# Half of a unit's gate-weighted one-hots are multiplied by their gates on ACT instead of DVE

## What is computed

```
idx = take(i1, ia) * 128 + take(i2, ib)            # (i, j) of each slot
gates = softmax(vals)
h = einsum('tkd,td->tk', expert_u[idx], x)
a = gelu(h) * gates
out = einsum('tk,tkd->td', a, expert_v[idx])
```

## Time and profile before

| | us |
|---|---|
| median of 3 runs (2219.46 to 2220.31) | 2220.23 |
| the profiled execution, its own time | 2217.2 |
| its span | 2215.4 |

### The profile page before, as it was taken

One profiled execution on the slowest core, in us unless ns is written; L12 is line 12 of the kernel. 1 busy time (PEld: TensorE's weight loads), 2 busy tenths in 40 slices (PEclk: granted clock), 3 DMA queues, 4 the chain that ended last, 5 costly groups with the idle time before them and its releaser, 6 DMA issues.

```text
span 2215.4 us, 35977 instructions
## 1 busy us (share of the span) xinstructions
PE 2127.0 (96%) x12658; PEld 1842.3 (83%) x12658; DVE 1250.9 (56%) x2110; ACT 977.1 (44%) x1406; POOL 126.1 (6%) x65
## 2 busy tenths in 40 slices
PE   7999996899999999999999999999999999999998
PEld 6998995656888888888888888787888888899997
DVE  4457799788666666666675333322645433355553
ACT  5644553223555555555564222212434334346652
POOL 0000676000000000000000000000000000000000
PEclk9999998999999999999999999999999999999999
DMA  6344453588555555556553333232233245254552
GB/s 220 125 133 162 135 169 114 201 292 275 191 191 188 189 186 186 188 203 194 188 173 116 98 100 99 95 100 90 78 112 112 85 143 174 100 186 138 185 188 96
DMA packets 95559, 343.24 MB, mean 155 GB/s; under 512 B 10915, under 2 KB 12451, under 8 KB 95109
## 3 DMA queue, kind: packets, MB, share of 16 engines
q1 hardware_dynamic: 94388, 337.28, 45.6%
q0 software_dynamic: 1104, 5.05, 0.6%
HBM read 341.24 MB, written 1.05 MB: 155 GB/s over the span
## 4 chain that ended last, share of the span: by engine, by line
PE 85%; DVE 10%; issue 2%; DMA 1%; ACT 1%; DVEq 0%; ACTq 0%; SPq 0%
PE ps L1418 14%; PE ps L1419 14%; PE ps L1420 14%; PE ps L1647 8%; PE ps L1661 5%; PE ps L1663 5%; PE ps L1662 5%; PE ps L1649 4%; PE ps L1449 2%; PE ps L1451 2%; PE ps L1450 2%; PE ps L1622 2%; PE ps L1598 1%; PE ps L1801 1%; DMA RAW<-in_wstream 1%
## 5 line engine op out<-in xcount | busy, mean ns | idle before, releaser
L832 DVE TENSOR_TENSOR WL<-RAW,WH 128x1024 fp32r<-128x1024 f32 x519 | 627.0, 1223 | 504.4 <-ACT WH L420 500.9
L420 ACT ACTIVATE WH<-RAW 128x1024 fp32r<-128x1024 f32 x565 | 585.0, 1053 | 285.8 <-PE ps L1420 159.7
L1418 PE MATMUL ps<-XH,WH 128*128 128x256 f32 (+1 forms) x1200 | 385.0, 321 | 7.0 <-DVE XL L849 5.3
L1419 PE MATMUL ps<-XL,WH 128*128 128x256 f32 (+1 forms) x1200 | 379.5, 316 | 0.0
L1420 PE MATMUL ps<-XH,WL 128*128 128x256 f32 (+1 forms) x1200 | 379.4, 316 | 0.0
L1647 PE MATMUL ps<-XHL,WH 128*128 128x512 f32 x752 | 268.5, 397 | 0.0
L1418 PEld LDWEIGHTS ps<-XH,WH 128*128 128x128 f32 x1200 | 229.3, 191 | 25.9 <-issue 5.4
L1419 PEld LDWEIGHTS ps<-XL,WH 128*128 128x128 f32 x1200 | 229.7, 191 | 15.5 <-issue 1.0
L1420 PEld LDWEIGHTS ps<-XH,WL 128*128 128x128 f32 x1200 | 229.6, 191 | 14.3
L1418 PE MATMUL ps<-XHL,WH 128*128 128x256 f32 x696 | 207.1, 298 | 24.9 <-POOL WL L391 11.4
L1649 PE MATMUL ps<-XHL,WL 128*128 128x256 f32 x752 | 210.9, 280 | 0.0
(11 more groups left out here) (276 smaller groups left out, 3153.1 us busy)
## 6 DMA issues: line engine op xcount, KB each, us to landing
RAW<-in_wstream SPq DMA_DIRECT2D x637, 512.0 KB, 3.4
H<-in_xT SPq DMA_DIRECT2D x1, 1024.0 KB, 4.8
CTX<-in_ctxT POOLq DMA_DIRECT2D x1, 1024.0 KB, 6.8
HX<-in_ctxT POOLq DMA_DIRECT2D x1, 1024.0 KB, 6.0
DIST<-in_dist POOLq DMA_DIRECT2D x1, 1024.0 KB, 5.1
out<-HX SPq DMA_DIRECT2D x2, 512.0 KB, 3.1
MASK<-in_mask POOLq DMA_DIRECT2D x1, 512.0 KB, 3.9
DFTL<-in_dftl POOLq DMA_DIRECT2D x1, 512.0 KB, 3.7
```

The source lines that it names most:

```text
L420: act.activation(WH[:, slot, :], RAW[:, slot, :], ACT.Copy).then_inc(hi_ready, 1)
L832: dve.tensor_tensor(WL[:, slot, :], RAW[:, slot, :], WH[:, slot, :].bitcast(F32), ALU.subtract).then_inc(lo_ready, 1)
L1418: pe.matmul(dst, wh, xh, start=start, stop=False, skip_group_check=not check)
L1419: pe.matmul(dst, wh, xl, start=False, stop=False, skip_group_check=not check)
```

## The change

A constant `FUSED = 4` splits a unit's 8 tokens. DVE still compares for `OJ`. For tokens 4 to 7 it then writes plain one-hots, 0 or 1, into `OI` with one compare of 512 elements and signals `hot_ready`; for tokens 0 to 3 it compares and multiplies as before and signals `onehot_ready`. ACT multiplies the four plain one-hots in place, each by its slot gates: four instructions (Copy with a scale per partition out of `SLT`), then `weighed`. This is `weigh(n)`. It stands on ACT ahead of the copy of the tables of the unit before: `weigh(0)`, `weigh(1)`, copy(0), `weigh(2)`, copy(1), and so on. PE waits for `weighed` of unit n as well.

```
+FUSED = 4
...
+            def weigh(n):
+
+                act.wait_ge(s["hot_ready"], n + 1)
+                for t in range(FUSED, 8):
+                    ins = act.activation(OI[n % 2][:, t, :], OI[n % 2][:, t, :], ACT.Copy,
+                                         scale=SLT[:, 2, 8 * n + t:8 * n + t + 1])
+                ins.then_inc(s["weighed"], 1)
+
             act.sem_inc(s["g_ready"], 2)
             done = 0
+            weigh(0)
             for n in range(UNITS):
+                if n + 1 < UNITS:
+                    weigh(n + 1)
                 act.wait_ge(s["onehot_used"], n + 3)
...
-                for t in range(8):
+                half = [P, 8 - FUSED, P]
+                dve.tensor_tensor(OI[q][:, FUSED:8, :], IOTA[:, :].unsqueeze(1).to_broadcast(half),
+                                  SLT[:, 0, 8 * n + FUSED:8 * n + 8].unsqueeze(2).to_broadcast(half),
+                                  ALU.is_equal).then_inc(s["hot_ready"], 1)
+                for t in range(FUSED):
...
                 pe.wait_ge(s["onehot_ready"], n + 1)
+                pe.wait_ge(s["weighed"], n + 1)
```

## The result

| | before | after |
|---|---|---|
| median, us (20 runs each) | 2219.85 (2214.83 to 2223.62) | 2223.04 (2220.39 to 2226.98) |
| the profiled execution, us | 2217.2 | 2222.95 |
| its span, us | 2215.4 | 2221.2 |
| the stage, from the last hidden copy to the first expert product, us | 405.79 to 539.82: 134.03 | 405.50 to 542.61: 137.11 |

The changed kernel takes 1.0017 of the time before, with a 95% interval of 1.001 to 1.0024: slower by a little, 0.17%, inside the 0.2% that were called "same" ahead. Forecast were 2224.2 us and 1.0018.

The account below looks back on a forecast made before the run. PE and its loads (4.10 us a unit) bound the stage; the change replaces them by an ACT and DVE loop of 4.20. +2.9 us, plus 1.1 for long loads, makes +4.0: 2224.2 us (1.0018), range 2220.6 to 2229.0.

Parts of the forecast that it names:

- What bounds the stage: Stage from 403 to 538 us: PE and its loads set 4.10 us a unit; DVE is busy but not waited for.
- DVE's own price: DVE before the change: eight L1111 in 2.13 us, own minimum 3.62 us a unit; the change saves 0.47 a unit.
- The price of a weighing: ACT's multiply of one one-hot by its gates: 0.29 us apart, four 1.16, or 1.26 with the last one's tail.
- the rival of 0.19 us: Cheap weighing on ACT: 0.19 us each, loop 3.80, below PE's 4.10; only the start stays, 2221 us; chance 0.16.
- The compare of four tokens: DVE's new compare of 512 elements: 0.68 us by itself, counted as 0.60 in a row of several.
- The loop: ACT and DVE wait for each other in the stage: 4.20 us a unit, 0.11 more with a row_sum.
- The rival of adding delays: In the stage, late loads for PE add to the ACT and DVE loop's delays: +8 us, 2228 us; chance 0.19.
- Start: Unit 0 on PE waits for the first weighings: starts at 407.4 us instead of 406.58, +0.8 us.
- End: Unit 31: OJ compare at 534.2 us, one-hots ready for PE at 537.4 against 534.50 before, +2.9 us.
- The term for long loads: Two long load legs in the stage stick out of the loop's slack by 1.2 and 0.4 us; +1.1 us taken.
- The absolute time: Whole kernel: profiled execution 2217.2 + 4.0 = 2221.2 us, median 3.0 above it, 2224.2 us (1.0018).
- What was costed at nothing: In the stage, PE's added wait, the MROW copy on ACT (0.60 us) and PE's clock (1.00) were priced at zero.

Follow-up runs that it names:

- DVE's part alone: Changed kernel without ACT's weighings and PE's wait for them, so four tokens' gates are left out: 0.9994 (0.9984 to 1.0003) of the time before, stage 132.35 us.
- the OI compare first: Changed kernel with DVE's four-token compare for OI ahead of the OJ compare: 1.0002 (0.9992 to 1.0013) of the time before, stage 134.79 us.
- `row_sum` moved: Kernel before with DVE's row_sum ahead of gated_rows instead of behind it: 1.0004 (0.9996 to 1.0013), stage 136.70 us.
- the kernel with both swaps: Changed kernel with the compare for OI ahead of the OJ compare and row_sum ahead of gated_rows: 0.9995 (0.9985 to 1.0006), stage 132.89 us.

## Why the prediction was right

**What bounds the stage.** Right for the units with chunks of w_ada. DVE was 92% busy, and relieving it alone gave 0.9994 (0.9984 to 1.0003), which isn't told from nothing. Units 30 and 31 have no chunks: there the chain of the kernel before in its first profile, from 527.74 to 534.46 us, is DVE's two rounds of OJ compare and eight L1111, and with DVE's part alone the last round took 3.10 us in place of 3.52. The forecast's sum holds this end too, since the loop sets it after the change.

**DVE's own price** was read 0.08 us too high. The 2.13 us for eight L1111 end at a `gated_rows` that started 0.03 us after ACT's copy ended; where it doesn't wait, they take 2.05 (414.48 to 416.53), 0.26 each and not 0.27. So DVE's own round was 3.52 us and not 3.62, and it saved 0.42 us a unit (3.52 to 3.10), some 14 us and not 15. The 3.16 us for the OI compare first (3.10 measured) and the 3.44 of DVE alone with two weighings (3.35) were too long for the same reason. As DVE alone doesn't bound the new loop, the forecast didn't suffer.

**The price of a weighing.** 0.29 us apart was forecast from L436 and L618. The four take 1.28 us to the end of the last against 1.26, and the copy starts 1.19 us after the first against 1.16. That is 0.30 us for one, and the rival of 0.19 us fell. A per-partition scale costs about what the forecast worked out for a bias. The estimate of 1.17 us from the Trainium skill ("ScalarE: Activation LUTs", section What ACT_TABLE_LOAD costs) agrees with these rows.

**The compare of four tokens.** 0.69 us long, the next one 0.60 later; forecast 0.68 and 0.60.

**The loop.** 4.20 us forecast, 4.20 measured, 4.29 with a `row_sum` against 4.31. The rival of adding delays fell: one of 29 rounds was longer than that (4.75) in the first profile and three in the second, 0.5 and about 1.0 us in all, where it had +8. The variants with three, five and six weighings came out as the same sum gave, 3.77, 4.62 and 5.05.

**Start.** Unit 0 was forecast at 407.4 and came at 407.14. Counted from ACT's last hidden copy, whose start lay 0.29 us earlier in this execution, that is 1.64 us against 0.79 before: the 0.8 of the sum.

**End.** The OJ compare of unit 31 was forecast at 534.2 and started at 534.09; unit 31 at 537.4 and at 537.32. The sum without its last term, +2.9, stands against +3.1 in the stage.

**The term for long loads was mis-sized.** 1.1 us were added for legs that the loop would not hide. Three legs of 4.79, 4.48 and 5.03 us are on the chain after, and they cost 0.46 us in one round (4.75 in place of 4.29, ahead of 508.62). From the third compare to the last the profile has 123.71 us, the loop alone gives 123.6. The second profile has no load on the chain at all. The reason for the term was weak too: that three timed runs lie within 0.04% was taken for loads that repeat, while 20 runs of the kernel before spread over 0.4%, and its stage over 2.6 us in two profiles.

**The absolute time** came out right to 1.2 us in part by luck. The forecast had 2221.2 us for the profiled execution and a median 3.0 above it; measured were 2222.95 and a median 0.1 above it, and the two misses nearly cancel. The profiled execution is 5.8 us longer than the one before, of which the stage has 3.1. Of the rest 2.4 us lie far behind it, in a stretch between two table loads of ACT (39.94 us before, 42.32 after) where the same PE work is granted a lower clock. In windows of it the granted clock, behind the busy times, is 0.92 after:

```profile
1573.60:1615.90 42.30, 38.63 (x204) 33.66 (x203) 18.89 (x26) 15.85 (x16) 0.00 (x0) 0.92 0.32 102
```

It is 1.00 in both profiles of the kernel before and in no other: with the OI compare first the stretch took 41.54 us at 0.96, and in the ten other profiles, `row_sum` moved and DVE's part alone among them, 42.3 to 42.7 at 0.92. Whether that is chance or comes with any edit stays open. It is hardly a steady cost, since the OI compare first, two weighings, DVE's part alone and the kernel with both swaps have medians within 1.1 us of the kernel before's, and the medians of the change differ by 3.2 us and not by 5.8.

**What was costed at nothing** held in the main. PE's wait for the weighings is 1.7 us at unit 0 and 1.63 at unit 31, both in the sum; between them it is 0.48 and 0.47 us at units 2 and 4 and 0.17 once more, off the chain. The MROW copies waited for PE for 2.9 us in all. The clock stayed at 1.00 in the first profile, but in the second it fell to 0.72 for 5 us, at a round 0.49 us too long; that much the forecast had left out.

## What to carry to other kernels

Taking work off a busy engine brings nothing if the engines behind it don't wait for that work. Before moving it to an idle engine, walk the round that it closes there: what stands behind it in that queue, who waits for that, and what that one does before it feeds the first again. If the sum is longer than the pace of what binds now, the move costs the excess in each round; if it can be brought under it, as here by issuing the compare that feeds the other engine first, it costs nothing.

## What the runs showed of the hardware

After an idle time of 3.3 us in a stage of loose PE work, the granted clock fell to a mean of 0.66 over 5 us, and 16 passes took 3.50 us in place of 2.02 to 2.05; after one of 2.2 us it was 0.94 and then 0.72 in stretches of 5 us, and they took 2.77. Far behind the stage the same PE work was granted 1.00 in both profiles of the kernel before and 0.92 to 0.96 in the eleven others, 1.6 to 2.8 us of time, with no edit near it. And loads of 512 KB through four slots at about 300 GB/s took 3.7 to 7.1 us on the chains; between two profiles of one kernel the stage's length differed by 2.6 us, and the loads on its chain by 3.9.
